# Projections with the token groups innermost: three PSUM banks in turn under one set of weights

## The reference

```python
h = rmsnorm(x, norm_mix_g[i])
q, k, v, pb = split_cols(h @ w_in_e[j], E_SPLITS)        # layer 0; layer 1: h @ w_in_o[j]
...                                                      # the mixers
x = x + jnp.concatenate([oa, ob], axis=-1) @ w_out_e[j]  # layer 1: w_out_o[j]
h = rmsnorm(x, norm_ffn_g[i])
xs[gi] = x + swiglu(h, ffn_w_gate[i], ffn_w_up[i], ffn_w_down[i])

def swiglu(h, wg, wu, wd):
    return (jax.nn.silu(h @ wg) * (h @ wu)) @ wd         # D_FF = 2816
```

## Time and profile before

| | us |
|---|---|
| median of 3 runs | 3547.99 (3541.64 to 3548.44) |
| the profiled execution | 3541.42 |
| its span | 3539.3 |
| TensorE busy | 3043.4 (86%), 23687 products |
| weight loads busy | 2794.3 (79%), 23687 loads |
| VectorE busy | 1411.3 (40%) |
| GpSimd busy | 1052.9 (30%) |
| ScalarE busy | 793.7 (22%) |

### The profile page before, as it was taken

How to read it: one execution, slowest core, us unless ns; L and a number is a source line. 1 busy time by engine, 2 the same in 40 slices (tenths; PEclk the granted TensorE clock), 3 DMA queues, 4 the chain that set the end, 5 groups by cost and what they waited for, 6 DMA issues and landing times.

```text
span 3539.3 us, 59907 instructions
## 1 busy us (share of the span) xinstructions
PE 3043.4 (86%) x23687; PEld 2794.3 (79%) x23687; DVE 1411.3 (40%) x2714; ACT 793.7 (22%) x1520; POOL 1052.9 (30%) x689
## 2 busy tenths in 40 slices
PE   5994866866889999999999996666679999999997
PEld 4994744744568999999999995343368999999997
DVE  5135555564862221121123113999942221121122
ACT  2002232231542212121122011222222212121121
POOL 3221000000024323232236214555634323232235
PEclk9997978988889999999999997777689999999998
DMA  3110000000021111111112112000021111111112
GB/s 112 42 47 16 3 2 2 3 2 18 0 74 36 36 54 43 46 42 42 48 42 98 44 46 82 0 0 0 0 75 36 36 54 43 47 42 42 48 42 68
DMA packets 51832, 133.70 MB, mean 38 GB/s; under 512 B 7128, under 2 KB 22104, under 8 KB 51432
## 3 DMA queue, kind: packets, MB, share of 16 engines
q1 hardware_dynamic: 51688, 131.61, 11.4%
HBM read 119.68 MB, written 11.92 MB: 37 GB/s over the span
## 4 chain that ended last, share of the span: by engine, by line
PE 78%; DVE 12%; issue 5%; ACT 2%; DMA 1%; DVEq 0%; POOL 0%; SPq 0%; POOLq 0%; ACTq 0%
PE PS L313 21%; PE PS L315 21%; PE PS L314 21%; PE PS L1291 2%; PE PS L822 2%; PE PS L1259 2%; DVE c_s L1477 2%; PE PS L923 1%; PE PS L1272 1%; PE PS L935 1%; PE PS L932 1%; PE PS L866 1%; DVE c_zc L1521 1%; PE PS L988 1%; PE PS L1537 1%
## 5 line engine op out<-in xcount | busy, mean ns | idle before, releaser
L313 PE MATMUL PS<-h_hi,w_hi 128*128 128x384 f32 (+1 forms) x3456 | 1135.0, 328 | 67.4 <-POOL w_lo L405 26.4
L314 PE MATMUL PS<-h_lo,w_hi 128*128 128x384 f32 (+1 forms) x3456 | 1132.8, 328 | 0.0
L315 PE MATMUL PS<-h_hi,w_lo 128*128 128x384 f32 (+1 forms) x3456 | 1132.6, 328 | 0.0
L405 POOL TENSOR_TENSOR w_lo<-w_raw,w_hi 128x1024 fp32r<-128x1024 f32 (+2 forms) x208 | 461.0, 2216 | 1123.9 <-ACT w_hi L383 1123.9
L313 PEld LDWEIGHTS PS<-h_hi,w_hi 128*128 128x128 f32 x3456 | 652.7, 189 | 68.9 <-issue 68.6
L314 PEld LDWEIGHTS PS<-h_lo,w_hi 128*128 128x128 f32 x3456 | 652.7, 189 | 0.3
L315 PEld LDWEIGHTS PS<-h_hi,w_lo 128*128 128x128 f32 x3456 | 652.5, 189 | 0.0
L383 ACT ACTIVATE w_hi<-w_raw 128x1024 fp32r<-128x1024 f32 (+2 forms) x208 | 201.8, 970 | 907.0 <-PE PS L315 907.0
L673 DVE TENSOR_TENSOR x<-PS,x 128x384 f32 (+1 forms) x240 | 128.4, 536 | 556.6 <-PE PS L315 551.8
L315 PE MATMUL PS<-hid_hi,w_lo 128*128 128x384 f32 (+1 forms) x1056 | 346.9, 329 | 0.0
L313 PE MATMUL PS<-hid_hi,w_hi 128*128 128x384 f32 (+1 forms) x1056 | 346.7, 328 | 0.0
(11 more groups left out here) (278 smaller groups left out, 3619.2 us busy)
## 6 DMA issues: line engine op xcount, KB each, us to landing
w_raw<-in_w_gu SPq DMA_DIRECT2D x88, 512.0 KB, 3.3
w_raw<-in_w_d SPq DMA_DIRECT2D x48, 384.0 KB, 3.1
w_raw<-in_w_e SPq DMA_DIRECT2D x20, 512.0 KB, 3.3
w_raw<-in_w_o SPq DMA_DIRECT2D x20, 512.0 KB, 3.2
x<-in_x SPq DMA_DIRECT2D x4, 1536.0 KB, 9.4
x_home<-x SPq DMA_DIRECT2D x1, 4352.0 KB, 12.7
w_raw<-in_w_oe SPq DMA_DIRECT2D x8, 512.0 KB, 3.2
w_raw<-in_w_d SPq DMA_DIRECT2D x16, 256.0 KB, 2.7
```

The source lines that it names most:

```text
L313: pe.matmul(out, w_h, a_h, start=k == 0, stop=False)
L314: pe.matmul(out, w_h, a_l, start=False, stop=False)
L315: last = pe.matmul(out, w_l, a_h, start=False, stop=k == kn - 1)
L405: pool.tensor_tensor(w_lo[slot][:, 0:kn, :], w_raw[slot][:, 0:kn, :], w_hi[slot][:, 0:kn, :].bitcast(F32), ALU.subtract).then_inc(sm["w_lo ...
```

## The change

The loop over groups moves from outside the slabs to the innermost place. For each slab and each of the three weight and activation pairs, the tile now issues the product of group 0, group 1 and group 2, one after the other, each into its own bank. The number, shapes and operands of the products are the same. The waits of all three groups (`evac_done` and `before(g)`) stand ahead of the first product, and the three increments of `product_done` sit on the tile's last three products.

```diff
             pe.wait_ge(sm["w_lo_ready"], n + 1)
-            for g, (c0, cn) in enumerate(GROUPS):
+            for g in range(NG):
                 if not (isinstance(n, int) and n < 2):
                     pe.wait_ge(sm["evac_done"], n * NG + (g + 1 - 2 * NG))
                 if before:
                     before(g)
-                out = PS[:, NG * slot + g, 0:cn]
-                for k in range(kn):
-                    w_h, w_l = w_hi[slot][:, k, :], w_lo[slot][:, k, :]
-                    a_h, a_l = hi[:, k, c0:c0 + cn], lo[:, k, c0:c0 + cn]
-                    pe.matmul(out, w_h, a_h, start=k == 0, stop=False)
-                    pe.matmul(out, w_h, a_l, start=False, stop=False)
-                    last = pe.matmul(out, w_l, a_h, start=False, stop=k == kn - 1)
-                last.then_inc(sm["product_done"], 1)
+            for k in range(kn):
+                w_h, w_l = w_hi[slot][:, k, :], w_lo[slot][:, k, :]
+                for i, (w, a) in enumerate(((w_h, hi), (w_h, lo), (w_l, hi))):
+                    for g, (c0, cn) in enumerate(GROUPS):
+                        last = pe.matmul(PS[:, NG * slot + g, 0:cn], w, a[:, k, c0:c0 + cn], start=k == 0 and i == 0,
+                                         stop=k == kn - 1 and i == 2)
+                        if k == kn - 1 and i == 2:
+                            last.then_inc(sm["product_done"], 1)
```

## The result

| | before | after |
|---|---|---|
| device time, median | 3548.22 us (3541.64 to 3549.2, 4 runs) | 3651.49 us (3646.99 to 3654.32, 4 runs) |
| ratio after / before | | 1.0294, 95% interval 1.0276 to 1.0312 |
| profiled execution, its span | 3541.42 us, 3539.3 | 3649.67 us, 3647.5 |
| mean granted clock of the span | 0.920 | 0.911 |

The change costs 103 us, 2.9%. The forecast was 3655 us, in a range from 3620 to 3690. Between the two profiled executions the span grows by 108.2 us, 5 us more than between the medians, because the profiled execution of the kernel before was shorter than its median.

What follows compares the result with a forecast made beforehand. The prediction took TensorE, at 78% of the span, its back-to-back work and its waits, to bound the kernel. 0 + 62 + 39 + 6 = 107 us, set on the median 3548.0, gave 3655 us, range 3620 to 3690.

Steps and rivals of the forecast that it cites:

- five starts on h_lo: Two output projections, two first gate stages and the second layer's input projection start later, waiting for all groups: 39 us.
- end of the kernel: After the last tile GpSimd squares three groups instead of one, ending 3.5 us later.
- two barriers: Behind the input projections, VectorE has two more evacuations (1.1 us) and two more conv groups (some 1.5 us).
- Part 1: Order of products inside a tile: repeated weights and turns to another bank both change nothing, 0 us.
- Part 2: End of a tile: three groups closing together stay covered by the next tile inside a stage, 0 us.
- rival 5: GpSimd is late in the last down stages, up to 8 us each, 3671 us; chance 6%.
- Part 3: Start of a stage: TensorE waits for all three groups; eight down stages cost 62 us, five other stages 39 us.
- Part 4: The ends: later last squares and more VectorE work before two barriers, together 6 us.
- Cheaper repeats (1): Products that repeat their weights save 120 us against 107 us of joints, giving 3535 us, faster; chance 4%.
- The clock that stays up (2): The clock stays up through gaps of 5.9 us before down stages, giving 3640 us; chance 14%.
- Hidden joints (3): TensorE begins with the first group, leaving only ends and slower h_lo, about 15 us: 3563 us; chance 2%.
- costly turns (4): Each turn between banks costs time, up to 180 us more, up to 3835 us; chance 4%.

Runs made afterwards that it cites:

- e5: The kernel before with its second and third product exchanged, so no product inside a slab repeats weights; 3546.01 us beside 3547.41 for the kernel before.
- e6: The changed kernel with another order inside a slab: a bank turn at every product, only 2 of 9 weights repeated; 3652.79 us.
- e2: The changed kernel with only the first tile of every stage run group by group as before; 3590.26 us, ratio 1.0128 to the kernel before.
- e3: The changed kernel with only the last tile of every stage run group by group as before; 3603.71 us, ratio 1.0165 to the kernel before.
- e4: The changed kernel with 25 dummy products before TensorE's wait at each of the eight down stages; 3631.35 us, ratio 1.0243 to the kernel before.
- e8: The changed kernel with grouped first and last tiles of stages, plus dummy products before first gate stages and output projections; 3532.47 us, ratio 0.9964 to the kernel before.
- e7: The changed kernel with turns between the two 384-column groups only, the 320-column group following alone; 3629.66 us.

## Why the prediction was right

The mechanism held for the terms that carry the sum: the waits at the joints, their causes, and the half clock behind them. The span grew by 108.2 us where the sum said 107, and the medians by 103. Term by term, durations of the two profiled executions:

| term | forecast, us | measured, us |
|---|---|---|
| products inside a stage, 208 tiles | 0 | -8 (-0.04 each, -0.02 in the 16 shortest) |
| eight gaps before down stages | 47 (5.9 each) | 49 (6.0 idle, 6.2 from start to start) |
| half clock behind them | 15 (1.9 each) | 21 (2.6 each) |
| five starts on h_lo | 39 | 39 |
| end of the kernel | 3.5 | 5.0 |
| two barriers | 2.6 | 2.4 |
| GpSimd in the last down stages | 0 | 1.3 |
| mixers behind the barriers | 0 | -1.5 |
| sum | 107 | 108 |

The mixers have the same instructions in both kernels. Their length varies from execution to execution: in e5, whose joints are those of the kernel before, the first layer's mixers took 3.8 us more than in the kernel before. So the -1.5 us is put down to chance and not to the change.

**Part 1** was right in its core: a turn costs nothing, a repeat saves nothing (e5, e6). Rows 4 read in hundredths couldn't show 0.56 ns per product. Its bound for cheaper repeats was miscounted: 7 products of 9 repeat their weights in the change, 10528 and not 9024, and 4512 do so in the kernel before. The -8 us and the -1.5 us nearly cancel against the terms that came out larger, 6 us of clock, 2 us in the gaps, 1.5 us at the end and 1.3 us of GpSimd. So it is partly luck that the total looks better than its parts.

**Part 2**, the cover inside a stage, held except in the last down stage of layer 0. There three tiles take 9.3 us and three 9.05, where the other stages of this size have 8.94. That is the mechanism of rival 5, at 1.3 us where it allowed 8. In that stage VectorE makes the next projection's h_lo beside GpSimd's squares, and the squares of a tile take 6.2 us (1908.84 to 1915.06) instead of the 5.44 of the forecast. In layer 1 no h_lo is made there, the squares take 5.4 us, and its tiles stay at 8.94.

**Part 3**, the gap: 5.9 us forecast, 5.99 us of idle time measured, with both of its causes shown apart by e2 and e3. The forecast counted the delay against the moment when the stage starts in the kernel before, and on that count it is 6.15 us. It also expected two multiplications to be slowed by up to 0.6 us each. One was, by 0.8 us, and one hid_lo took 1.31 us instead of 1.0. The mis-sized term is the clock. I took 1.9 us between 1.5 and 2.3, from gaps that stood between other kinds of work. Here the low clock reached 5.4 to 5.6 us into dense products in all eight stages, and the first tile lost 2.6 us, near the upper bound of 2.7. e4 takes the low clock away and measures 2.5.

The five starts: +7.2 and +7.0 us before the output projections, +10.3 twice before the first gate stages (8.7 to 19.05), +3.0 before the second layer's input projection (1.31 to 4.28), whose first tile took 1.5 us longer. The clock's part at the other four changed by between +0.5 and -0.9 us, -0.5 in all. The 24 h_lo took 17.2 us, as forecast. These sizes come from comparing each start with the one of before, and e2 and e3 show the shares of start and end for the two kinds.

**Part 4**: GpSimd's last squares end 3.5 us later, as forecast. The reduction behind them then ran at clock 0.52, which I had not counted, 4.00 us instead of 2.43.

**The rivals.** Cheaper repeats (1) fall by e5 and e6. The clock that stays up (2) falls for gaps of 6 us, eight of eight, while of 2.8 us gaps it is true for three in eight, and of 3.3 us gaps for none in eight. Hidden joints (3) and costly turns (4) fall by the waits and the windows above. GpSimd late (5) is there at 1.3 us.

## What to carry to other kernels

Before loops are exchanged so that several accumulators close together, read what starts behind the last of them. In this kernel the loss was at the joints of stages, one evacuation chain each, and inside a stage it was nothing but for 1.3 us in one down stage. If an order is wanted for the inside, keep the group-by-group order in the first and last tile of each stage. A wait of TensorE costs its length and can cost the half clock behind it: 2.6 us behind each wait of 6.0 us here, 1.6 to 2.8 us behind five of eight waits of 2.8 us. Where real work can't be had, products that nobody reads held the clock, in e4 and in e8.

## What the runs showed of the hardware

- The weight load of a product that repeats its weights is issued and takes 189 ns like any other, and the step from product to product doesn't change, whether 3 products of 9 repeat or none (before, e5), or 7 of 9 or 2 (after, e6).
- Products of 384, 384 and 320 columns in turn over three banks take 1.6 ns less per three than products sorted by size, 0.04 us of 11.84 in a tile. Turns between two banks with one size have no price and no gain (e7).
- Behind a gap of 6.0 us in dense work the granted clock was at 1.2 GHz every time, for 5.4 to 5.6 us of products. Behind gaps of 3.3 us it fell in eight cases of eight (e7), behind gaps of 2.8 us in five of eight, in e2 and in e3.
- A VectorE multiplication of 128x384 took 0.56 us alone and 1.38 beside a GpSimd operation, more than the 1.15 seen before. It is so in all 44 up tiles of the changed kernel: the second multiplication starts just behind a hid_lo of 1.0 us and takes 1.18 to 1.38 us.
